# Summing the last 512 columns of the PEER value rows on TensorE

## The chip, the core and the metric

One Trainium2 chip, one of its cores. TensorE (PE) multiplies matrices into PSUM, its accumulation memory of eight banks of 512 fp32 columns; VectorE (DVE) and ScalarE (ACT) compute along the free dimension of 128 partitions; GpSimd (POOL) issues the gathers from HBM, SyncE (SP) the plain loads. All transfers share 16 DMA engines. The metric is the device time of one launch in microseconds (us), the median of three runs.

## The reference

Two layers, an S5 mixer and an RG-LRU mixer, each followed by a PEER channel mixer, over 256 prompt tokens and 32 sample tokens with 2048 channels, all in fp32. The part that matters here is the PEER mixer. Each token picks, in 8 heads, 16 of 16384 experts by product keys, and each expert is one row `u` and one row `v` of 2048:

```python
idx, g = peer_retrieve(hf, w_q, sub_keys)          # 8 heads x 16 experts, softmax weights
u = u_emb[ib]
act = jnp.einsum("nd,nhkd->nhk", xb, u)            # a dot product per expert
wgt = jax.nn.gelu(act, approximate=False) * gb
v = v_emb[ib]
out = jnp.einsum("nhk,nhkd->nd", wgt, v)           # a weighted sum of value rows
```

## The kernel before

**Tiles.** The tokens lie in three tiles: 0 and 1 are the 128-token halves of the prompt, 2 holds the 32 sample tokens, each on four partitions. A token of tiles 0 and 1 has 128 experts (PICKS) on its own partition; a sample token's 128 experts are shared out over its four copies, 32 on each, and `sample_sum` adds the copies on TensorE afterwards.

**Gathers.** POOL gathers one row of 2048 fp32 for each of the 128 partitions at a time (an indirect DMA, 1 MB) into a ring of eight slots (`ring`, in the tensor `arena`). `rounds` (L487) loops over rounds of eight gathers; slot r is filled anew when the semaphore `row_used[r]` tells that VectorE has used it. Each layer has 144 dot rows and 144 value rows in each of two halves: 288 gathers per table and layer, 1152 in all.

**Stages.** VectorE goes through the rows in one fixed order: dot rows of tiles 0 and 2, value rows of tiles 0 and 2, dot rows of tile 1, value rows of tile 1, all of layer 0; then the same for layer 1. A dot row (`u_row`, L1494) is one instruction of 2048 columns. A value row (`v_row`, L1509) multiplies the gathered row by the token's weight and adds the running sum, which lies in PSUM banks 4 to 7 (`high_banks`); each waits for the one before it, by `row_used`.

**What runs between the rows.** `Turns` counts VectorE's rows and runs other work at fixed row numbers. Two chains of work take the RG-LRU layer and the second layer's retrieval along under the rows of the PEER mixer: `first_chain` (tiles 0 and 2) under the dot rows and value rows of layer 0's tile 1, `second_chain` (tile 1) under layer 1's dot rows of tiles 0 and 2 (160 rows) and the value rows after them. The tables at the top of the file give the row numbers: NORM_ROW for the norm ahead of the queries, CHOOSE_ROW for choosing experts (`chain_choose`, three parts, two rows apart), SOFT_ROW for the softmax. Choosing takes the sixteen best of each key list and then of their sums, and turns them into expert numbers.

**TensorE.** It runs the chain's products as soon as their inputs are there (`chain`): gates and recurrence inputs, output rows (`token_rows`), then the 16 query products and four blocks of scores (`pair_scores`). The weights come as slabs of 1 MB through a ring of four slots (`W`); SP loads a slot anew when the product that read it is done. TensorE has no part in the value rows.

**Clock.** The profile's PEclk is the granted TensorE clock: 1.0 is 2.4 GHz and 0.5 is 1.2 GHz, and a stretch shows the mean.

## Time and profile before

| | us |
|---|---|
| median of 3 runs (4014.38 to 4015.89) | 4015.09 |
| the profiled execution | 4012.11 |
| its span in the profile | 4010.2 |
| VectorE busy, 84% of the span | 3371.5 |
| GpSimd busy, 39% | 1552.0 |
| TensorE busy, 30% | 1221.7 |
| ScalarE busy, 11% | 460.3 |
| bytes moved, over the whole span | 1404 MB, 350 GB/s |

The span runs from the first instruction to the last; the execution's time has 1.9 us around it. The first 690 us are the S5 layer and the first retrieval, with few transfers; from there to the end the eight slots are filled without a pause in the program. The stages in the trace, by the lines of VectorE's rows: value rows of layer 0, tiles 0 and 2, from 1121 to 1518; dot rows of tile 1 with the first chain from there to 1946; value rows of tile 1 to 2372; dot rows of layer 1 with the second chain to 2891; value rows of tiles 0 and 2 to 3374; dot rows of tile 1 to 3684; value rows of tile 1 to the end. An engine's busy share over the whole span mixes these stages, so the windows by stage are the view to read. In them the DMA column is the mean busy share of the 16 DMA engines (1.01 is full) and GB/s what they moved.

### The profile page before, as it was taken

The page shows a single profiled execution, that of the slowest core. Times are in us where ns is not written, and L with a number is a line of the kernel's source. Part 1 is how long each engine was busy: PE and PEld are TensorE (multiplying, and loading weights), DVE is VectorE, ACT ScalarE, POOL GpSimd, SP SyncE. Part 2 cuts the span into 40 slices and gives each one's busy share as a digit, 9 for nine tenths or more (in the row PEclk, how much of TensorE's full clock was granted, in tenths as well). Part 3 has the DMA queues.
Part 4 walks back from the last instruction along what each step waited for, and adds up shares of the span by engine and source line. Part 5 has one row for each costly group of instructions (what it writes and reads, how often), then busy time and mean ns, then how long its engine had stood idle before and what let it go on. Part 6 is the DMA issues. An engine that isn't in the chain of part 4 may idle for free.

```text
span 4010.2 us, 25596 instructions
## 1 busy us (share of the span) xinstructions
PE 1221.7 (30%) x7394; PEld 1015.7 (25%) x7394; DVE 3371.5 (84%) x3564; ACT 460.3 (11%) x917; POOL 1552.0 (39%) x2027
## 2 busy tenths in 40 slices
PE   4666999000000007659370026470051000000000
PEld 2333778000000006559260026460051000000000
DVE  6777026999999998896889997868979999999998
ACT  6554021000000002120000002100000000000000
POOL 5999003543433343222322342223422334434332
PEclk8878999555555558779685558785576555555555
DMA  1001335899999999999996999999997999999998
GB/s 69 13 10 51 111 126 189 334 421 399 427 427 427 427 427 407 426 426 426 419 426 237 411 423 425 427 426 426 427 427 273 374 420 417 427 427 428 427 428 367
DMA packets 197389, 1404.25 MB, mean 350 GB/s; under 512 B 21952, under 2 KB 26304, under 8 KB 26768
## 3 DMA queue, kind: packets, MB, share of 16 engines
q0 software_dynamic: 167008, 1215.18, 72.7%
q1 hardware_dynamic: 30000, 187.74, 11.6%
q8 instruction: 47, 0.77, 0.1%
q14 instruction: 46, 0.38, 0.0%
q10 hardware_dynamic: 288, 0.18, 0.0%
HBM read 1399.77 MB, written 3.24 MB: 350 GB/s over the span
## 4 chain that ended last, share of the span: by engine, by line
DVE 50%; DMA 28%; POOL 7%; PE 7%; issue 7%; ACT 1%; POOLq 0%; DVEq 0%; ACTq 0%
DVE ps L1509 30%; DMA arena<-in_u_dram,ixs 24%; DVE arena L1494 13%; DMA arena<-in_v_dram,ixs 4%; PE ps L604 3%; POOL arena L423 2%; PE ps L644 2%; POOL arena L426 1%; POOL arena L430 1%; POOL arena L431 1%; POOL arena L404 1%; DVE arena L1389 1%; DVE arena L1382 1%; POOL arena L427 1%; DVE arena L1383 1%
## 5 line engine op out<-in xcount | busy, mean ns | idle before, releaser
L1494 DVE CUSTOM_DVE_ANT_0 arena<-arena,ps 128x2048 f32<-128x2048 f32 x556 | 1254.9, 2285 | 184.8 <-DMA arena<-in_u_dram,ixs 170.3
L1509 DVE SCALAR_TENSOR_TENSOR ps<-arena,ps 128x2048 f32<-128x2048 f32 x564 | 1327.9, 2354 | 90.5 <-DMA arena<-in_v_dram,ixs 29.8
L497 POOL DMA_INDIRECT arena<-in_v_dram,ixs x576 | 566.1, 983 | 1025.7 <-DVE ps L1509 960.2
L497 POOL DMA_INDIRECT arena<-in_u_dram,ixs x560 | 545.1, 973 | 1056.4 <-DVE arena L1494 983.2
L762 PE MATMUL ps<-HT,W 128*128 128x160 f32 (+1 forms) x3072 | 407.6, 296 | 62.5 <-ACT HN L1108 28.7
L762 PEld LDWEIGHTS ps<-HT,W 128*128 128x128 f32 x3072 | 401.1, 199 | 68.6 <-issue 47.2
L741 PE MATMUL ps<-ident,HN 128*128 128x128 f32 (+1 forms) x96 | 18.8, 377 | 1304.0 <-DVE HN L1237 1304.0
L741 PEld LDWEIGHTS ps<-ident,HN 128*128 128x128 f32 (+1 forms) x96 | 15.6, 217 | 1307.8 <-DVE HN L1237 1306.2
L1331 DVE TENSOR_TENSOR_SCAN arena<-arena 128x256 f32<-128x256 f32 x128 | 84.3, 717 | 67.9 <-POOL arena L451 65.9
L710 PE MATMUL ps<-HN,arena 128*32 128x256 f32 x512 | 140.9, 443 | 0.0
L790 PE MATMUL ps<-W,arena 128*128 128x128 f32 x1024 | 125.4, 284 | 44.8 <-DVE arena L1605 20.4
L790 PEld LDWEIGHTS ps<-W,arena 128*128 128x128 f32 x1024 | 121.9, 199 | 47.2 <-DVE arena L1605 20.6
L644 PE MATMUL ps<-HT,W 128*128 128x288 f32 x512 | 126.7, 409 | 0.0
L669 PE MATMUL ps<-HN,repsum 128*128 128x512 f32 x16 | 11.8, 898 | 371.5 <-DVE HN L1509 370.1
L604 PE MATMUL ps<-arena,W 128*128 128x288 f32 x512 | 124.4, 406 | 0.8 <-ACT arena L938 0.8
L863 ACT ACTIVATE HN<-X 128x2048 f32<-128x2048 f32 x15 | 28.5, 1902 | 823.2 <-DVE X L1509 810.4
L1371 DVE TENSOR_TENSOR arena<-arena 128x288 f32 x16 | 7.3, 459 | 131.1 <-ACT arena L1007 131.1
L423 POOL TENSOR_TENSOR arena<-arena 128x32 f32<-128x32 f32 (+1 forms) x256 | 107.7, 451 | 8.9 <-POOL arena L431 8.9
L644 PEld LDWEIGHTS ps<-HT,W 128*128 128x128 f32 x512 | 97.7, 192 | 27.6 <-issue 1.0
L604 PEld LDWEIGHTS ps<-arena,W 128*128 128x128 f32 x512 | 97.2, 190 | 27.7 <-issue 1.0
L669 PEld LDWEIGHTS ps<-HN,repsum 128*128 128x128 f32 x16 | 4.2, 282 | 378.1 <-issue 373.7
L774 PE MATMUL ps<-HN,W 128*128 128x160 f32 (+1 forms) x256 | 53.6, 379 | 101.1 <-ACT HN L1120 99.3
(245 smaller groups left out, 2171.2 us busy)
## 6 DMA issues: line engine op xcount, KB each, us to landing
W<-in_slabs_dram SPq DMA_DIRECT2D x168, 1024.0 KB, 10.8
arena<-in_u_dram,ixs POOLq DMA_INDIRECT x576, 16.5
arena<-in_v_dram,ixs POOLq DMA_INDIRECT x576, 14.3
GB<-in_norms_dram POOLq DMA_DIRECT2D x4, 1024.0 KB, 6.0
arena<-in_s_bc_dram SPq DMA_DIRECT2D x32, 128.0 KB, 2.1
X<-in_x_dram SPq DMA_DIRECT2D x3, 1024.0 KB, 10.8
out_y_dram<-HN SPq DMA_DIRECT2D x2, 1024.0 KB, 6.6
arena<-in_keys_dram POOLq DMA_DIRECT2D x1, 1024.0 KB, 5.2
```

What stands on the lines that cost most here:

```text
L404: ins = nc.gpsimd.tensor_tensor(t[n], b[c], f[e], ALU.mult)
L423: ins = nc.gpsimd.tensor_tensor(t[n], a[c], s[e], ALU.mult)
L497: pool.indirect_dma_start(ring[:, r, :], None, table, bass.IndirectOffsetOnAxis(ap=ixs[:, side, r:r + 1], axis=0)).then_inc(row_in[r], 16)
L604: mm = nc.tensor.matmul(ps[:, r % 2, 0:NT], W[:, slot, P * k:P * (k + 1)], rhs[:, k, :], start=(k == 0), stop=(k == KT - 1))
L644: mm = nc.tensor.matmul(ps[:, r % 2, 0:NT], W[:, slot, P * k:P * (k + 1)], HT[:, k, :], start=(k == 0), stop=(k == KT - 1))
L710: nc.tensor.matmul(ps[rows, 5, 0:SEQ], c, PR[n][:, q, :], start=False, stop=(n == 3), skip_group_check=True)
L762: mm = nc.tensor.matmul(ps[:, bank, 0:CHAIN_COLS[c]], W[:, slot, P * k:P * (k + 1)], HT1[c][:, k, :], start=(k == 0), stop=(k == KT - 1))
L774: mm = nc.tensor.matmul(ps[:, bank, 0:CHAIN_COLS[c]], W[:, slot, at:at + P], XC[c][g % 2][:, 2 * (b // 4) + e, :], start=(e == 0), stop=(e ...
L790: mm = nc.tensor.matmul(ps[:, bank, out], Y[:, k, :], W[:, slot, P * k:P * (k + 1)], start=(k == 0), stop=(k == KT - 1))
L1331: ins = V.tensor_tensor_scan(dst[:, q, :], dec[:, bass.ds(k * QK + q, 1)].to_broadcast([P, SEQ]), src[:, q, :], 0.0, ALU.mult, ALU.add)
L1494: V.tensor_tensor_reduce(ring[:, r, :], ring[:, r, :], token, 1.0, 0.0, ALU.mult, ALU.add, AV[:, COL_AT[t] + n:COL_AT[t] + n + 1]).then_in ...
L1509: V.scalar_tensor_tensor(to, ring[:, r, :], weight, total, ALU.mult, ALU.add).then_inc(row_used[r], 1)
```

## The change

VectorE's value row is cut to the first 1536 columns (OWN). For the other 512, VectorE writes the token's weight on the diagonal of a 128 x 128 matrix (DG, three buffers, from `ident`), and TensorE multiplies that matrix with the row's last 512 columns and accumulates in PSUM bank 7 over all rows of a tile (`value_rows`). At a tile's end VectorE adds the bank to X or copies it to ACC (`last_columns`), and `v_done` takes the place of the last `row_used` for those who wait for the sum.

A slot may now be filled only when both engines have read it, so POOL waits for `row_used[r]` and `row_pe[r]` in value rounds (`value_rounds`). Ahead of the dot rounds that follow value rows it waits once for all eight `row_pe` (`values_read`), at three places.

On TensorE the value rows stand in one instruction order with the chain: the query products of a chain, with their transposes and scores, are taken out of `chain` and placed between value rows by a `Turns` of TensorE's own (TURN_ROW). CHOOSE_ROW and SOFT_ROW move to later rows and further apart.

```diff
+OWN = D - BANK
+DIAGS = 3
+PHASES = [(0, 0), (0, 2), (0, 1), (1, 0), (1, 2), (1, 1)]
-NORM_ROW = [132, 172]
-CHOOSE_ROW = [[150, 158, 166, 174, 180], [190, 198, 206, 214]]
-SOFT_ROW = [192, 224]
+NORM_ROW = [132, 168]
+TURN_ROW = [6, 10]
+CHOOSE_ROW = [[158, 170, 182, 194, 202], [196, 208, 220, 232]]
+SOFT_ROW = [212, 244]
...
+def values_before(layer, t):
+    return sum(PICKS_OF[u] for _, u in PHASES[:PHASES.index((layer, t))])
...
+            def value_rounds(layer, t):
+                start, at = ROUNDS * layer + V_AT[t], ROUNDS * layer + V_AT[t] - COL_AT[t] // RING
+                before = values_before(layer, t) // RING
+                with pool.Fori(start // 2, start // 2 + PICKS_OF[t] // RING // 2) as i:
+                    for side in range(2):
+                        indices(at, i, side)
...
+                        for r in range(RING):
+                            pool.wait_ge(row_used[r], i * 2 + side)
+                            pool.sem_inc(gather_go, 1)
+                            pool.wait_ge(row_pe[r], i * 2 + (side + before + 1 - start))
+                            pool.sem_inc(gather_go, 1)
+                            issue(experts_v[layer], i, side, r)
+
+            def values_read(rounds):
+                for r in range(RING):
+                    pool.wait_ge(row_pe[r], rounds + 1)
...
+            value_rounds(0, 0)
+            value_rounds(0, 2)
+            values_read(values_before(0, 1) // RING)
+            dot_rounds(experts_u[0], U_AT[1] - PITCH // RING, U_AT[1], V_AT[1])
+            value_rounds(0, 1)
...
+            def chain_queries(c):
+                yield TURN_ROW[c]
                 if c == 0:
                     turned(8, 0)
+                    yield TURN_ROW[c] + 2
                     turned(9, 2)
...
                 for p in range(4):
                     for i in range(4):
+                        yield TURN_ROW[c] + 6 + 3 * (4 * p + i)
                         chain_product(c, LOAD_Q + 4 * p + i, MM_Q + 4 * p + i)
                         if i == 0 and p > 0:
                             pair_scores(c, p - 1)
+                yield TURN_ROW[c] + 6 + 3 * 16
                 pair_scores(c, 3)
...
+            def value_rows(layer, t, turns):
+                first = values_before(layer, t)
+                if first > 0:
+                    pe.wait_ge(v_done, PHASES.index((layer, t)))
+                for n in range(PICKS_OF[t]):
+                    R, r = ROUNDS * layer + V_AT[t] + n // RING, n % RING
+                    pe.wait_ge(diag_set, first + n + 1)
+                    pe.wait_ge(row_in[r], 16 * (R + 1))
+                    nc.tensor.matmul(ps[:, 7, :], DG[(first + n) % DIAGS], ring[:, r, OWN:D], start=(n == 0),
+                                     stop=(n == PICKS_OF[t] - 1)).then_inc(row_pe[r], 1)
+                    turns.row()
...
             chain(0)
+            turns = Turns(chain_queries(0))
+            value_rows(0, 1, turns)
+            turns.finish()
...
             def v_row(layer, t, n):
...
+                v = values_before(layer, t) + n
+                if v >= DIAGS:
+                    dve.wait_ge(row_pe[(v - DIAGS) % RING], (v - DIAGS) // RING + 2)
+                V.tensor_scalar(DG[v % DIAGS], ident[:], weight, None, ALU.mult).then_inc(diag_set, 1)
                 dve.wait_ge(row_in[r], 16 * (R + 1))
...
+                row = ring[:, r, 0:OWN]
...
-                V.scalar_tensor_tensor(to, ring[:, r, :], weight, total, ALU.mult, ALU.add).then_inc(row_used[r], 1)
+                V.scalar_tensor_tensor(to, row, weight, total, ALU.mult, ALU.add).then_inc(row_used[r], 1)
+
+            def last_columns(layer, t):
+                dve.wait_ge(row_pe[RING - 1], (values_before(layer, t) + PICKS_OF[t]) // RING + 1)
+                if t == 2:
+                    V.tensor_copy(ACC[:, OWN:D], ps[:, 7, :]).then_inc(v_done, 1)
+                else:
+                    V.tensor_tensor(X[:, t, OWN:D], ps[:, 7, :], X[:, t, OWN:D], ALU.add).then_inc(v_done, 1)
```

Three places in the order of instructions show what moves. The first is TensorE at the end of the first chain (HT and W are the chain's tokens and the weight slabs, `arena` with 128x512 a ring slot's last columns). Before, after the transposes:

```order
L741 MATMUL ps<-ident,HN 128x128 x16
L741 MATMUL ps<-ident,HN 128x32 x16
L762 MATMUL ps<-HT,W 128x160 x80
L806 MATMUL ps<-HT,arena 128x128
L808 MATMUL ps<-HT,arena 32x128
```

And now:

```order
L905 MATMUL ps<-arena 128x512 x6
L783 MATMUL ps<-ident,HN 128x128 x16
L905 MATMUL ps<-arena 128x512 x2
L783 MATMUL ps<-ident,HN 128x32 x16
L905 MATMUL ps<-arena 128x512 x4
L804 MATMUL ps<-HT,W 128x160 x16
L905 MATMUL ps<-arena 128x512 x3
L804 MATMUL ps<-HT,W 128x160 x16
L905 MATMUL ps<-arena 128x512 x3
```

Five query products stood in one run of 80 matmuls; now one of 16 comes after every three value rows.

The second place is VectorE at the start of a tile's value rows, with the waits of each instruction (`arena` is the slot, X the first running sum, `ident` the source of the diagonal). Before:

```order
L1509 SCALAR_TENSOR_TENSOR ps<-arena,X 128x2048 [waits row_in0,vstep]
L1509 SCALAR_TENSOR_TENSOR ps<-arena,ps 128x2048 [waits row_used0,row_in1]
L1509 SCALAR_TENSOR_TENSOR ps<-arena,ps 128x2048 [waits row_used1,row_in2]
L1509 SCALAR_TENSOR_TENSOR ps<-arena,ps 128x2048 [waits row_used2,row_in3]
L1509 SCALAR_TENSOR_TENSOR ps<-arena,ps 128x2048 [waits row_used3,row_in4]
```

And now, in layer 0's tile 1:

```order
L1587 TENSOR_SCALAR arena<-ident,arena 128x128 [waits row_pe5,vstep]
L1597 SCALAR_TENSOR_TENSOR ps<-arena,X 128x1536 [waits row_in0]
L1587 TENSOR_SCALAR arena<-ident,arena 128x128 [waits row_pe6]
L1597 SCALAR_TENSOR_TENSOR ps<-arena,ps 128x1536 [waits row_used0,row_in1]
L1587 TENSOR_SCALAR arena<-ident,arena 128x128 [waits row_pe7]
L1597 SCALAR_TENSOR_TENSOR ps<-arena,ps 128x1536 [waits row_used1,row_in2]
```

Ahead of each sum stands a diagonal, which waits for TensorE's product of three rows earlier and not for its own row.

The third place is POOL between the last value rows and the next dot rows, here at the end of layer 1's tile 2. Before:

```order
L497 DMA arena<-in_v_dram,ixs 128x2048 [waits row_used7]
L489 REGISTER_ALU
L489 COMPARE_AND_BRANCH
L489 UNCONDITIONAL_BRANCH [waits chain_picks]
L489 ISA
L484 COPY ixs<-arena 128x8
L492 ISA
L497 DMA arena<-in_u_dram,ixs 128x2048 [waits index_set,row_used0]
L497 DMA arena<-in_u_dram,ixs 128x2048 [waits row_used1]
```

And now:

```order
L502 DMA arena<-in_v_dram,ixs 128x2048 [waits row_used7,row_pe7]
L521 REGISTER_ALU
L521 COMPARE_AND_BRANCH
L507 UNCONDITIONAL_BRANCH [waits row_pe4,row_pe3,row_pe5,row_pe2,row_pe6,row_pe1,row_pe7,row_pe0,chain_picks]
L507 ISA
L497 COPY ixs<-arena 128x8
L510 ISA
L502 DMA arena<-in_u_dram,ixs 128x2048 [waits index_set,row_used0]
L502 DMA arena<-in_u_dram,ixs 128x2048 [waits row_used1]
```

The first dot gather, which waited for its own slot alone, now stands behind TensorE's reads of all eight.

## Rows read from the trace of the kernel before

**Rows 1.** The page's chain of waits, part 4: shares of the span by engine.

```profile
DVE 50%; DMA 28%; POOL 7%; PE 7%; issue 7%; ACT 1%; POOLq 0%; DVEq 0%; ACTq 0%
```

**Rows 2.** Windows by stage: busy us per engine, PEclk, DMA share, GB/s.

```profile
1121.00:1518.00 397.00, 3.64 (x16) 3.00 (x16) 379.80 (x169) 5.94 (x9) 155.79 (x179) 0.50 1.01 427
1526.00:1946.00 420.00, 294.35 (x2192) 289.79 (x2192) 349.89 (x464) 64.58 (x181) 119.36 (x134) 0.84 1.01 421
1946.00:2372.00 426.00, 96.21 (x608) 87.19 (x608) 392.97 (x448) 15.69 (x34) 140.29 (x151) 0.60 0.92 377
2372.00:2891.00 519.00, 215.61 (x1680) 208.65 (x1680) 417.66 (x444) 65.43 (x148) 165.11 (x180) 0.72 1.01 426
2891.00:3374.00 483.00, 71.37 (x561) 69.29 (x562) 439.44 (x408) 16.03 (x33) 163.91 (x180) 0.57 0.93 382
...
3684.00:3994.00 310.00, 0.00 (x0) 0.00 (x0) 295.91 (x127) 0.05 (x1) 119.15 (x136) 0.50 1.01 426
```

**Rows 3.** Instruction groups: busy us, mean ns of one; idle before, releasers.

```profile
L1509 DVE SCALAR_TENSOR_TENSOR ps<-arena,ps 128x2048 f32<-128x2048 f32 x564 | 1327.9, 2354 | 90.5 <-DMA arena<-in_v_dram,ixs 29.8 <-DVE arena L1389 5.1 <-DVE ps L1509 2.8
L1494 DVE CUSTOM_DVE_ANT_0 arena<-arena,ps 128x2048 f32<-128x2048 f32 x556 | 1254.9, 2285 | 184.8 <-DMA arena<-in_u_dram,ixs 170.3 <-DVE arena L1429 0.2
...
L1338 DVE SCALAR_TENSOR_TENSOR HN<-arena 128x1024 f32<-128x1024 f32 x16 | 20.4, 1278 | 0.0
```

**Rows 4.** VectorE's timeline, a choice of experts: start us, us, line, operation.

```profile
2067.98 0.89 DVE L1379 MAX8 arena<-ps 128x8 f32<-128x128 f32 x4
...
2073.86 4.82 DVE L1509 SCALAR_TENSOR_TENSOR ps<-arena,ps 128x2048 f32<-128x2048 f32 x2 [0.31 <-DVE arena L1389]
2078.59 0.19 DVE L1413 CAST arena<-arena 128x64 f32<-128x64 uint32 x1
...
2084.25 4.82 DVE L1509 SCALAR_TENSOR_TENSOR ps<-arena,ps 128x2048 f32<-128x2048 f32 x2 [0.22 <-DVE arena L1389]
2088.98 0.17 DVE L1420 TENSOR_SCALAR arena<-arena 128x32 uint32<-128x32 uint32 x1
...
2093.55 9.72 DVE L1509 SCALAR_TENSOR_TENSOR ps<-arena,ps 128x2048 f32<-128x2048 f32 x4
```

**Rows 5.** Line L1557 (ns min/median/max), then the timeline of all engines there.

```profile
L1557 DVE TENSOR_SCALAR HN<-HN,CH x32: 333/343/499, 1564.1 to 2564.0; 128x128 f32<-128x128 f32 x32
...
1564.13 0.34 DVE L1557 TENSOR_SCALAR HN<-HN,CH 128x128 f32<-128x128 f32 x1
1564.39 0.30 DVE L1561 TENSOR_SCALAR HN<-HN,CH 128x32 f32<-128x32 f32 x1
...
1565.02 0.95 POOL L497 DMA_INDIRECT arena<-in_u_dram,ixs  x1 [3.97 <-DVE arena L1494]
```

**Rows 6.** TensorE's timeline (PE, PEld): sums of the samples, then query products.

```profile
3373.69 3.52 PE L669 MATMUL ps<-HN,repsum 128*128 128x512 f32 x4 [307.49 <-DVE HN L1509]
3378.63 1.98 PE L669 MATMUL ps<-HN,repsum 128*128 128x512 f32 x4 [1.41 <-DVE X L1540]
...
3373.66 0.50 PEld L669 LDWEIGHTS ps<-HN,repsum 128*128 128x128 f32 x2 [307.76 <-issue]
...
2038.72 17.65 PE L762 MATMUL ps<-HT,W 128*128 128x160 f32 x128
...
2930.40 18.13 PE L762 MATMUL ps<-HT,W 128*128 128x128 f32 x160 [0.69 <-ACT HT L1086]
```

**Rows 7.** A refill by POOL (timeline), landing times of gathers, windows after value stages.

```profile
1520.93 0.19 POOL L484 COPY ixs<-arena 128x8 int32 x1
...
1522.04 0.97 POOL L497 DMA_INDIRECT arena<-in_u_dram,ixs  x1 [0.91 <-POOL ixs L484]
...
DMA to landing us min/median/max: 5.4/16.0/36.3
...
1530.00:1550.00 20.00, 15.31 (x100) 15.10 (x101) 19.96 (x19) 2.44 (x14) 9.73 (x10) 0.74 0.90 333
3390.00:3410.00 20.00, 0.00 (x0) 0.00 (x0) 19.96 (x19) 0.00 (x0) 9.30 (x9) 0.50 0.97 386
```

More of the change, by code:

```diff
@@ L232, in hybrid_step @@
         cube = [P, PAIR, TOPK, TOPK]
+        OH1 = view(RING * D + 10 * PITCH + 40 + 256, 2 * PAIR * CANDS)
+        DG = [view(at - 512 + P * n, P) for n in range(DIAGS)]
         LIN = view(at, 512)
@@ L293, in hybrid_step @@
         row_used = [sem(f"row_used{r}") for r in range(RING)]
+        row_pe = [sem(f"row_pe{r}") for r in range(RING)]
+        diag_set, v_done = sem("diag_set"), sem("v_done")
         hn_set, index_set, gather_go = sem("hn_set"), sem("index_set"), sem("gather_go")
@@ L485, in indices, with issue, dot_rounds @@
                                       ).then_inc(index_set, 1)
-            def rounds(table, at, start, end):
+            def issue(table, i, side, r):
+                pool.indirect_dma_start(ring[:, r, :], None, table,
+                                        bass.IndirectOffsetOnAxis(ap=ixs[:, side, r:r + 1], axis=0)).then_inc(row_in[r], 16)
+            def dot_rounds(table, at, start, end):
                 with pool.Fori(start // 2, end // 2) as i:
@@ L496, in rounds @@
                             pool.sem_inc(gather_go, 1)
[L497 to L499 removed]
+                            issue(table, i, side, r)
+            def value_rounds(layer, t):
[4 more added lines that the diff above has]
+                        indices(at, i, side)
+                        pool.wait_ge(index_set, i * 2 + (side + 1))
+                        pool.sem_inc(gather_go, 1)
[3 more added lines that the diff above has]
+                            pool.wait_ge(row_pe[r], i * 2 + (side + before + 1 - start))
+                            pool.sem_inc(gather_go, 1)
+                            issue(experts_v[layer], i, side, r)
+            def values_read(rounds):
+                for r in range(RING):
+                    pool.wait_ge(row_pe[r], rounds + 1)
             def one_head(h, par):
@@ L839, in chain, with sample_turn @@
                             pair_scores(c, p - 1)
+                yield TURN_ROW[c] + 6 + 3 * 16
                 pair_scores(c, 3)
-            turned(6, 0)
+            def sample_turn():
+                yield 8
+                turned(6, 0)
+            def value_rows(layer, t, turns):
[9 more added lines that the diff above has]
+                    turns.row()
+            value_rows(0, 0, Turns(()))
+            turns = Turns(sample_turn())
+            value_rows(0, 2, turns)
+            turns.finish()
             pe.wait_ge(norm_ht, 28)
@@ L846, in _ @@
             chain(0)
+            turns = Turns(chain_queries(0))
+            value_rows(0, 1, turns)
+            turns.finish()
             turned(10, 1)
             chain(1)
+            turns = Turns(chain_queries(1))
+            value_rows(1, 0, turns)
+            turns.finish()
+            value_rows(1, 2, Turns(()))
             pe.wait_ge(key_used, 2 + HEADS + 8)
             sample_sum(1)
+            value_rows(1, 1, Turns(()))
         @block.scalar
@@ L1181, in _ @@
             chain_queries(0)
-            token_bank(0, ROUNDS, 9)
+            act.wait_ge(v_done, 3)
+            token_bank(0, 9)
             square(10, 1)
@@ L1210, in _ @@
             st = Steps()
+            for r in range(RING):
+                dve.sem_inc(row_pe[r], 1)
             dve.sem_inc(key_used, 2)
@@ L1503, in v_row @@
                     dve.wait_ge(row_used[(n - 1) % RING], ROUNDS * layer + V_AT[t] + (n - 1) // RING + 1)
+                row = ring[:, r, 0:OWN]
                 if n == 0 and t == 2:
-                    V.tensor_scalar(high_banks, ring[:, r, :], weight, None, ALU.mult).then_inc(row_used[r], 1)
+                    V.tensor_scalar(high_banks[:, 0:OWN], row, weight, None, ALU.mult).then_inc(row_used[r], 1)
                     return
-                total = X[:, t, :] if n == 0 else high_banks
-                to = high_banks if n < PICKS_OF[t] - 1 else ACC if t == 2 else X[:, t, :]
-                V.scalar_tensor_tensor(to, ring[:, r, :], weight, total, ALU.mult, ALU.add).then_inc(row_used[r], 1)
+                total = X[:, t, 0:OWN] if n == 0 else high_banks[:, 0:OWN]
+                to = high_banks[:, 0:OWN] if n < PICKS_OF[t] - 1 else ACC[:, 0:OWN] if t == 2 else X[:, t, 0:OWN]
+                V.scalar_tensor_tensor(to, row, weight, total, ALU.mult, ALU.add).then_inc(row_used[r], 1)
[5 more added lines that the diff above has]
+                    V.tensor_tensor(X[:, t, OWN:D], ps[:, 7, :], X[:, t, OWN:D], ALU.add).then_inc(v_done, 1)
             def u_rows(layer, t, turns, hn_count):
```

64 lines of the change are left out of this document (32 added, 32 removed).

## The prediction, made before the changed kernel was run

> **What bounds the kernel now.** I read the chain of waits first, then the busy times stage by stage, and only then single instructions. The chain gives half of the span to VectorE and 28% to transfers, and its largest piece is the value row on L1509 [rows 1]. Taken alone that promises much for a shorter value row. The stages say otherwise [rows 2]. One gathered row is 128 x 2048 x 4 bytes = 1.0486 MB; at 427 GB/s it takes 2.456 us. In the first value stage (1121 to 1518) the transfer engines are busy throughout at 427 GB/s, in the last one (3684 to 3994) at 426, and in the stages of dot rows and recurrence (1526 to 1946, 2372 to 2891) at 421 and 426. There a faster VectorE can only wait longer for rows.
>
> Two stages are different: 1946 to 2372 moved 377 GB/s and 2891 to 3374 moved 382. In bytes not moved that is (1 - 377/427) x 426 = 49.9 us and (1 - 382/427) x 483 = 50.9 us, **100.8 us** together. In them VectorE chooses experts between value rows. One choice has three parts; their starts and the starts of the next value rows give 5.88 + 5.66 + 4.57 = 16.1 us [rows 4]. The value row itself has no slack to pay for that: it lasts 2.354 us [rows 3], and four in a row take 9.72, a pitch of (9.72 - 2.35)/3 = 2.456 us [rows 4], exactly a row's transfer. So five choices (80.5 us) and four choices (64.4 us) come out as lost transfer, less what lies ready in the ring of eight: 80.5 - 49.9 = 30.6 and 64.4 - 50.9 = 13.5 us. The first also contains the last weight slabs, which moved while VectorE was late; the second holds few of them. I take the ring alone as 11 us (8 to 17; eight rows less the one in use are 17).
>
> **The change, part by part.** *Shorter value row.* From 1024 columns (1.278 us) to 2048 (2.354 us) an element costs 1.051 ns [rows 3]; 1536 columns give 1.278 + 512 x 1.051 = 1.816 us. The added diagonal is a TENSOR_SCALAR of 128 x 128 with a weight per partition. Its nearest rows are the 32 on L1557: median 343 ns, and the next instruction starts 0.26 us after one starts [rows 5]. The old pitch contains 0.10 us in which a row waits for its predecessor's result; the diagonal now stands in that gap. Without such a wait the next instruction started 4.73 us after the first of two value rows, so 4.73 - 2.456 = 2.27, or 0.08 before the row's end [rows 4]. New pitch: 1.816 - 0.08 + 0.26 = **2.00 us**. Lower bound: the old gap, with the diagonal wholly inside, 1.92. Upper bound: nothing overlaps, 1.816 + 0.343 + 0.10 = 2.26. I take 2.00, because both instructions on L1557's stretch overlap in that way.
>
> That leaves 2.456 - 2.00 = 0.456 us a row for choosing. *Choices spread out.* In the first chain they start at value row 30 and the softmax is at 84 (turn rows 158 and 212, less the 128 dot rows); the query products on TensorE stand at value rows 12, 15, ..., 57, and each frees a slot for one slab. Ten slabs are moved from row 30 on, 24.6 us of transfer during which VectorE may lag. Loss: 80.5 - 54 x 0.456 - 24.6 - 11 = 20.3 us. In the second chain (160 dot rows ahead) it is rows 36 to 84 and five slabs: 64.4 - 48 x 0.456 - 12.3 - 11 = 19.2 us. Together 39.5, plus 6 for TensorE's share of the pace (below): 46 instead of 100.8, a gain of **55 us**. With 1.92 and a cushion of 17 the two losses fall to 10 and 9 (a gain of 81); with 2.26 they are 34 and 32 (a gain of some 29 after TensorE's 6).
>
> *A barrier for the gathers.* Before, a slot's first dot row was issued as soon as that slot's value row was used. Now POOL waits, at three places, until TensorE has read the last value row, and all eight gathers of the next stage stand behind that wait; the dot rows on VectorE wait for them. When the last value row has landed nothing is in flight. TensorE's product of 512 columns takes 1.76 us at the slower level (3.52 for two) and 0.99 at the faster, with weights ahead of it (two loads in 0.50) [rows 6]: about 2.0. Then come POOL's index copy and its wait, 1.1 us, and the issue, 0.97 [rows 7]. The shortest landing was 5.4 us from issue; less 0.97 for issuing and 2.456 for moving, 2.0 us pass before data flows [rows 7]. Idle transfer: 2.0 + 1.1 + 1.0 + 2.0 = 6.1 us, three times, 18. Two of these places already lose (1 - 333/427) x 20 = 4.4 and (1 - 386/427) x 20 = 1.9 us, since VectorE stalls there on sums of the samples [rows 7]; that stall now lies beside the refill. Net cost 12 us (8 to 18).
>
> *TensorE's rows.* 576 products of at most 1.76 us plus weights lie inside a row's 2.456 us and beside VectorE's 1.82. The diagonal is built before the row lands, so both engines start at landing, and the slot comes free no later than before (2.35). Nothing for this, except where query products stand between. VectorE may build three diagonals ahead; if TensorE falls further behind, the fourth waits, and behind it on VectorE the sum and any choice, for which POOL waits in turn.
>
> *Query products in line.* A product of the first chain takes 17.65/4 = 4.41 us at the faster level, of the second 18.13/5 = 3.63 [rows 6]. Twelve value rows and four products make 12 x 1.27 + 17.6 = 32.9 us of TensorE in the first chain, against 16 transfers x 2.456 = 39.3: it fits, with the score products narrowly (hence the 6 us). *Ends of stages.* The last 512 columns are added by one 0.69 us instruction; it is exposed only at the very end, some 1 us.
>
> *A rule against the change.* L1557's instructions ran while POOL issued a gather (0.95 us from 1565.02); the longest of the 32 took 499 ns, and POOL's issue stayed at its usual length [rows 5]. The Trainium skill, "SBUF — State Buffer", section "Who interferes with whom", says that a tensor_scalar can take a two-port mode on ports shared with GpSimd, and that whichever issues first blocks the other fully. By the rows an encounter costs up to 0.16 us; by the rule it could cost the whole issue, and the sum would be rival 3's.
>
> **Sum.** Profiled execution: 4012.1 us (span 4010.2). 4012.1 - 55 + 12 + 1 = 3970; the median of the three runs is 3.0 above the profiled one, so **3973 us**, 1.0% faster. What a measurement can tell from no change is 0.2%, 8 us.
>
> **Rivals.**
> 1. *The spreading hides nearly all choices.* With pitch 1.92 and the full ring the gain is 81, the barriers cost 8: 4015 - 81 + 8 + 1 = 3943. For it: VectorE's idle time before rows is small, so whatever is saved is used. Against it: from row 60 on no slabs come, and two choices plus softmax stand in 24 rows, with 11 us of slack.
> 2. *TensorE becomes the bound, slower than before.* Its queue is in order: a value row stands behind each query product. At the slower level twelve rows and four products take 12 x 2.0 + 35.3 = 59.3 us in the first chain and 24 + 29.0 = 53 in the second, against 39.3. Over 48 rows each that loses 80 and 55 us, less two cushions, and the choices after row 60 still cost about 30: 143 in place of 100.8. With the barriers 4015 + 42 + 12 = 4069. In time at the slower level s, the first chain is late from (39.3 - 32.9)/26.4 = a quarter; the run turns slower than before at about six tenths. For it: in the two stages the granted clock was 0.60 and 0.57. Against it: there TensorE was busy 96 of 426 us; in 1526 to 1946 it was busy 294 of 420 and got 0.84 [rows 2], and value rows make this stretch denser still, the more so the slower it runs.
> 3. *POOL's issue holds up every diagonal.* If each waited 0.95 us, the pitch would be 2.95, above the transfer, in all 576 rows: 576 x 0.49 = 282 us and about 4300. The 499 ns above speak against it; a smaller dose (pitch 2.26) ends near 4015 - 29 + 12 + 1 = 3999.
> 4. *All 576 rows pay.* 576 x 0.456 = 263 us would give 3752. The 427 GB/s of the pure value stages exclude it, as bytes are unchanged.
>
> **How the numbers follow.** Forecast (3955 to 3990) 0.60; rival 1 0.12; pitch near 2.26, 3990 to 4010, 0.10, nearly all of it faster; gain eaten up by barriers and TensorE together, within 8 us of 4015, 0.05; rival 2 0.11; rival 3 in full 0.02. Faster 0.80, same 0.06, slower 0.14. The range runs from rival 1 to the dear diagonal, 3937 to 4012; outside lie rivals 2 and 3, most of the no-change case and a tail below, 0.2 in all.
>
> **What the profile after would show.** Value rows of 1.82 us and diagonals of about 0.34; a pitch near 2.0 where choices stand, still 2.456 in the first and last value stages; 405 GB/s or more in the two stages of choices; three gaps of about 6 us in the gathers ahead of dot rows, with POOL waiting for TensorE; TensorE at the faster level between value rows 12 and 60. The forecast is wrong if VectorE waits there for TensorE's products (rival 2), if diagonals take 0.5 us or more (rival 3), or if the gaps last beyond 10 us.

## The result, and the profile after

The changed kernel takes 3975.24 us (median of four runs, 3974.68 to 3975.65), against 4014.74 for the kernel before beside it: a ratio of 0.9903 (0.9886 to 0.992), 1.0% faster. The profiled execution's span fell from 4010.2 to 3973.2 us. The forecast was 3973.

The chain of waits has turned round. Where VectorE held 50% and transfers 28% [rows 1], the page after shows this (part 4, then part 5's group of the new value row: busy us, mean ns of one, idle before and its releaser):

```profile
DMA 50%; DVE 24%; PE 11%; POOL 7%; issue 7%; ACT 1%; POOLq 0%; DVEq 0%; ACTq 0%
...
L1597 DVE SCALAR_TENSOR_TENSOR ps<-arena,ps 128x1536 f32<-128x1536 f32 x564 | 1027.9, 1823 | 207.3 <-DMA arena<-in_v_dram,ixs 206.9
```

The value row lasts 1.823 us where it was 2.354 [rows 3], and of its 207.3 us of idle time 206.9 are waits for a row. Two value rows and the diagonal between them on VectorE's timeline, ahead of the third part of a choice:

```profile
2072.46 1.81 DVE L1597 SCALAR_TENSOR_TENSOR ps<-arena,ps 128x1536 f32<-128x1536 f32 x1
2074.19 0.28 DVE L1587 TENSOR_SCALAR arena<-ident,arena 128x128 f32<-128x128 f32 x1
2074.39 1.82 DVE L1597 SCALAR_TENSOR_TENSOR ps<-arena,ps 128x1536 f32<-128x1536 f32 x1
```

The second sum starts 1.93 us after the first (2.456 before [rows 4]): the diagonal starts 0.09 before the sum ends and the next sum 0.20 after the diagonal.

The stages, in windows as in [rows 2] (us; busy us of PE, PEld, DVE, ACT, POOL; PEclk, DMA share, GB/s): a stage of value rows alone, then the two stages with choices, and between them a piece of the first:

```profile
1122.00:1505.00 383.00, 278.65 (x328) 69.73 (x328) 316.16 (x321) 5.66 (x8) 148.66 (x171) 0.64 1.01 427
1965.00:2337.00 372.00, 266.10 (x856) 139.17 (x856) 324.49 (x558) 15.65 (x34) 124.19 (x138) 0.76 0.97 397
2190.00:2250.00 60.00, 30.61 (x36) 8.20 (x36) 57.54 (x122) 0.34 (x1) 17.95 (x20) 0.64 0.76 283
2880.00:3313.00 433.00, 301.90 (x872) 135.90 (x872) 372.45 (x560) 15.50 (x32) 155.24 (x172) 0.77 0.98 409
```

Value rows alone run at 427 GB/s as before. The stages with choices went from 377 and 382 to 397 and 409. In transfer not done that is (1 - 397/427) x 372 = 26.1 and (1 - 409/427) x 433 = 18.3 us, 44.4 in place of 100.8: a gain of 56.4. What is left lies close together: 2190 to 2250 lost (1 - 283/427) x 60 = 20.2 us, the first chain's last two choices and its softmax.

The three joints between value rows and dot rows, and the end (same columns), of after and then of before:

```profile
1505.00:1560.00 55.00, 34.99 (x152) 23.93 (x151) 43.96 (x44) 7.04 (x22) 23.98 (x24) 0.72 0.83 346
2337.00:2390.00 53.00, 30.46 (x174) 23.43 (x173) 40.32 (x38) 9.25 (x19) 25.99 (x23) 0.67 0.89 369
3313.00:3370.00 57.00, 15.37 (x16) 4.14 (x16) 44.52 (x44) 5.37 (x5) 24.57 (x24) 0.54 0.88 364
3940.00:3973.20 33.20, 16.15 (x19) 3.89 (x18) 21.17 (x21) 3.49 (x4) 1.89 (x2) 0.60 0.59 249
```

```profile
1510.00:1560.00 50.00, 31.64 (x182) 27.44 (x183) 46.06 (x41) 7.84 (x28) 21.57 (x20) 0.73 0.96 388
2365.00:2390.00 25.00, 5.47 (x33) 4.87 (x34) 24.65 (x20) 7.78 (x10) 14.31 (x11) 0.56 1.00 409
3370.00:3410.00 40.00, 5.51 (x8) 1.85 (x8) 39.07 (x36) 5.37 (x5) 19.03 (x18) 0.59 0.99 406
3977.00:4010.20 33.20, 0.00 (x0) 0.00 (x0) 24.49 (x13) 3.49 (x4) 1.89 (x2) 0.50 0.58 244
```

They lose 10.4, 7.2 and 8.4 us, 26.0 together, where the kernel before lost 4.6, 1.1 and 2.0: 18.4 us more. The end loses 13.8 instead of 14.2. Sum: 4010.2 - 56.4 + 18.4 - 0.4 = 3971.8, and the span is 3973.2. The 1.4 us left fit a later start: the first dot row begins at 696.75 where it began at 694.68.

Inside the second joint (all engines; the last value row, its product, POOL's index copy and first gather; then windows of 1 us):

```profile
2345.53 1.81 DVE L1597 SCALAR_TENSOR_TENSOR X<-arena,ps 128x1536 f32<-128x1536 f32 x1 [0.43 <-DMA arena<-in_v_dram,ixs]
...
2345.64 1.10 PE L905 MATMUL ps<-arena 128*128 128x512 f32 x2 [0.46 <-DMA arena<-in_v_dram,ixs]
2347.09 0.19 POOL L497 COPY ixs<-arena 128x8 int32 x1 [17.23 <-PE ps L905]
...
2348.18 0.96 POOL L502 DMA_INDIRECT arena<-in_u_dram,ixs  x1 [0.90 <-POOL ixs L497]
```

```profile
2343.00:2344.00 1.00, 0.80 (x1) 0.50 (x2) 0.91 (x1) 0.00 (x0) 0.00 (x0) 0.50 0.47 197
2344.00:2345.00 1.00, 1.00 (x2) 0.00 (x0) 1.00 (x2) 0.00 (x0) 0.00 (x0) 0.51 0.06 25
...
2349.00:2350.00 1.00, 0.00 (x0) 0.00 (x0) 0.00 (x0) 1.00 (x2) 0.70 (x2) 0.50 0.25 49
2350.00:2351.00 1.00, 0.00 (x0) 0.00 (x0) 0.00 (x0) 1.00 (x1) 0.69 (x2) 0.50 0.93 188
```

The transfers fall off at 2343.5, two microseconds before the last value row can start at 2345.53. The 25 GB/s after that are a sixteenth of 427: in the trace's packet records one of the 16 engines runs on after the others, with one packet of 8 KB every 0.31 us until 2345.18, and the last value row starts 0.35 us later. The first packets of the dot rows begin at 2349.85, 1.67 us after the issue at 2348.18, and between 2350 and 2351 the transfers still run at 188 GB/s.

### The profile page after: what moved, and what is told of

It reads as the page before. It is cut to its first block, busy times and chain, and to the rows that moved or that the text cites. A ratio compares the mean times of both kernels' runs of the same rounds, so it can differ in the third digit from the quotient of the medians.

```text
span 3973.2 us, 29731 instructions
## 1 busy us (share of the span) xinstructions
PE 2155.2 (54%) x8546; PEld 1261.4 (32%) x8546; DVE 3169.4 (80%) x4146; ACT 459.7 (12%) x917; POOL 1547.0 (39%) x2027
## 3 DMA queue, kind: packets, MB, share of 16 engines
q1 hardware_dynamic: 30000, 187.74, 11.7%
## 4 chain that ended last, share of the span: by engine, by line
DMA 50%; DVE 24%; PE 11%; POOL 7%; issue 7%; ACT 1%; POOLq 0%; DVEq 0%; ACTq 0%
DMA arena<-in_u_dram,ixs 26%; DMA arena<-in_v_dram,ixs 23%; DVE arena L1577 12%; DVE ps L1597 6%; PE ps L646 3%; PE ps L905 3%; POOL arena L436 3%; PE ps L686 2%; POOL arena L439 1%; POOL arena L444 1%; PE ps L804 1%; POOL arena L443 1%; DVE arena L1472 1%; DVE arena L1465 1%; DVE arena L1466 1%
## 5 line engine op out<-in xcount | busy, mean ns | idle before, releaser
L905 PE MATMUL ps<-arena 128*128 128x512 f32 x1152 | 943.6, 923 | 1367.2 <-DVE arena L1587 1096.1
L1597 DVE SCALAR_TENSOR_TENSOR ps<-arena,ps 128x1536 f32<-128x1536 f32 x564 | 1027.9, 1823 | 207.3 <-DMA arena<-in_v_dram,ixs 206.9
L502 POOL DMA_INDIRECT arena<-in_v_dram,ixs x576 | 557.9, 969 | 959.6 <-PE ps L905 656.7
L905 PEld LDWEIGHTS ps<-arena 128*128 128x128 f32 x1152 | 241.3, 258 | 2030.0 <-DVE arena L1587 1417.9
L804 PE MATMUL ps<-HT,W 128*128 128x160 f32 (+1 forms) x3072 | 420.0, 300 | 74.8 <-ACT arena L1187 32.0
L804 PEld LDWEIGHTS ps<-HT,W 128*128 128x128 f32 x3072 | 415.8, 203 | 101.1 <-issue 85.2
L1587 DVE TENSOR_SCALAR arena<-ident,arena 128x128 f32<-128x128 f32 x576 | 164.5, 286 | 9.7 <-PE ps L905 5.8
L436 POOL TENSOR_TENSOR arena<-arena 128x32 f32<-128x32 f32 (+1 forms) x256 | 116.6, 485 | 8.9 <-POOL arena L444 8.9
L686 PEld LDWEIGHTS ps<-HT,W 128*128 128x128 f32 x512 | 97.9, 192 | 27.6 <-issue 1.0
L744 PE MATMUL ps<-HT,arena 128*128 (+1 forms) x32 | 19.4, 710 | 129.1 <-POOL arena L444 129.1
```

Of the source, the lines that this page charges most:

```text
L436: ins = nc.gpsimd.tensor_tensor(t[n], a[c], s[e], ALU.mult)
L502: pool.indirect_dma_start(ring[:, r, :], None, table, bass.IndirectOffsetOnAxis(ap=ixs[:, side, r:r + 1], axis=0)).then_inc(row_in[r], 16)
L686: mm = nc.tensor.matmul(ps[:, r % 2, 0:NT], W[:, slot, P * k:P * (k + 1)], HT[:, k, :], start=(k == 0), stop=(k == KT - 1))
L804: mm = nc.tensor.matmul(ps[:, bank, 0:CHAIN_COLS[c]], W[:, slot, P * k:P * (k + 1)], HT1[c][:, k, :], start=(k == 0), stop=(k == KT - 1))
L905: nc.tensor.matmul(ps[:, 7, :], DG[(first + n) % DIAGS], ring[:, r, OWN:D], start=(n == 0), stop=(n == PICKS_OF[t] - 1)).then_inc(row_pe[r ...
L1587: V.tensor_scalar(DG[v % DIAGS], ident[:], weight, None, ALU.mult).then_inc(diag_set, 1)
```

## The experiments

Each was run beside the kernel before; ratios are to it, with their 95% interval, and differences are taken from medians.

### The new row numbers alone

```diff
 (kernel before)
-NORM_ROW = [132, 172]
-CHOOSE_ROW = [[150, 158, 166, 174, 180], [190, 198, 206, 214]]
-SOFT_ROW = [192, 224]
+NORM_ROW = [132, 168]
+CHOOSE_ROW = [[158, 170, 182, 194, 202], [196, 208, 220, 232]]
+SOFT_ROW = [212, 244]
```

> The kernel before with nothing but the new row numbers of NORM_ROW, CHOOSE_ROW and SOFT_ROW; VectorE keeps all 2048 columns. My theory: a value row of 2.456 us pitch leaves nothing over for choices, wherever they stand, and only the ring and the slabs hide some of them. The two stages lose about 101 us of transfer as before: 4015 us (4007 to 4023). Rival, the spreading is what gained the 56 us and TensorE's columns are a bystander: the losses fall to some 45 us and the time to about 3959.

Measured: 4020.65 us, ratio 1.0017 (1.0008 to 1.0027). The windows of its two stages, in the profiled execution (4013.71 us, the fastest of ten):

```profile
1962.00:2373.00 411.00, 99.56 (x608) 89.30 (x608) 372.56 (x432) 13.19 (x31) 130.50 (x143) 0.60 0.91 368
2895.00:3373.00 478.00, 70.03 (x560) 68.07 (x560) 436.28 (x405) 15.03 (x30) 163.54 (x179) 0.57 0.93 383
```

They lose 56.8 + 49.3 = 106 us, no less than before, and the median is 7 us longer. Spreading without a shorter value row gains nothing.

### The widest table alone

```diff
 (kernel before)
+NORM_ROW = [132, 168]
+CHOOSE_ROW = [[154, 166, 182, 204, 226], [190, 204, 222, 256]]
+PART_ROWS = [[4, 5, 7, 7, 8], [4, 5, 8, 8]]
+SOFT_ROW = [248, 284]
...
-                yield row + 2
+                yield row + PART_ROWS[c][step]
...
-                yield row + 4
+                yield row + 2 * PART_ROWS[c][step]
```

> The kernel before with the widest table of all: choices at 26, 38, 54, 76, 98 and 30, 44, 62, 96, their parts 4 to 8 rows apart; VectorE keeps all 2048 columns, and the slotwise refill is what that kernel has anyway. With 1536 columns on VectorE the same table ran in 3925 us. My theory: at a pitch of 2.456 us, equal to the transfer, the ring is empty after the first choice and nothing fills it again but the slabs, so the distance between choices is worth nothing: 4015 us (4007 to 4024), some 100 us lost in the two stages. Rival, a full ring ahead of each part hides it and the table alone gives most of the gain: 3960 or less.

Measured: 4020.97 us, ratio 1.0019 (1.001 to 1.0029). This is the table with which the fastest kernel below runs.

```profile
1962.00:2373.00 411.00, 100.60 (x608) 90.34 (x608) 372.99 (x434) 15.68 (x34) 130.96 (x143) 0.60 0.92 371
2895.00:3373.00 478.00, 72.62 (x560) 70.50 (x560) 435.03 (x408) 15.72 (x32) 162.75 (x179) 0.57 0.94 383
```

53.9 + 49.3 = 103 us lost: the two wider tables gain no more than the old one. A pitch equal to the transfer leaves nothing with which to fill the ring again.

### TensorE's columns with the choices close together

```diff
 (changed kernel)
-NORM_ROW = [132, 168]
-CHOOSE_ROW = [[158, 170, 182, 194, 202], [196, 208, 220, 232]]
-SOFT_ROW = [212, 244]
+NORM_ROW = [132, 172]
+CHOOSE_ROW = [[150, 158, 166, 174, 180], [190, 198, 206, 214]]
+SOFT_ROW = [192, 224]
...
-                        yield TURN_ROW[c] + 6 + 3 * (4 * p + i)
+                        yield TURN_ROW[c] + 6 + 2 * (4 * p + i)
...
-                yield TURN_ROW[c] + 6 + 3 * 16
+                yield TURN_ROW[c] + 6 + 2 * 16
```

> The changed kernel with its choices as close as they stood before: the old NORM_ROW, CHOOSE_ROW and SOFT_ROW, and the query products two value rows apart where they were three, so that the scores are there in time. My theory: TensorE's columns give the slack of 0.536 us a row, the rows between the first choice and the softmax say how much of it is used; 12 and 14 rows fewer cost 0.536 x 26 = 14 us, less what slabs that come closer together hide: 3986 us (3978 to 3996). Rival, the spreading carries most of the gain, slack or not: the losses go back to about 100 us and the time to 4015 or more, since the barriers stay. A second rival, TensorE's queue with denser query products becomes the bound: VectorE waits for products, 4000 or more, with the waits for TensorE named in the trace.

Measured: 3991.33 us, ratio 0.9945 (0.9928 to 0.9961).

```profile
1970.00:2350.00 380.00, 280.84 (x857) 136.05 (x858) 323.31 (x558) 15.66 (x34) 125.02 (x136) 0.76 0.95 386
2892.00:3330.00 438.00, 311.08 (x870) 131.63 (x870) 371.97 (x561) 15.71 (x32) 154.33 (x172) 0.74 0.97 403
```

The stages lose 36.5 + 24.6 = 61.1 us, 16.7 more than in the changed kernel, and the time is 16.1 longer. So of the gain of 56.4 us about 40 come with the choices as close as before, and 17 with the new distances of choices and query products, those only on top of the shorter row.

Not all of the 17 is shown to be distance between choices. The product of three rows earlier held up four diagonals for 7.1 us in all, against 5.8 in the changed kernel. But VectorE also waited for scores (us in total, times, longest):

```profile
DVE arena L1462 <- PE ps L850: 11.9, 3, 6.1
```

Three choices of the first chain were held up until TensorE had finished their scores, at 2040, 2074 and 2109; in the changed kernel none was. That stage loses 10.4 us more than in the changed kernel, and how much of this the late scores cost stays open: here the second rival is partly at work. The second stage has no such wait and loses 6.3 us more.

### A dearer diagonal

```diff
 (changed kernel)
+                if v >= 1:
+                    dve.wait_ge(extra_set, v)
+                V.tensor_scalar(zeros[:], zeros[:], weight, None, ALU.mult).then_inc(extra_set, 1)
                 V.tensor_scalar(DG[v % DIAGS], ident[:], weight, None, ALU.mult).then_inc(diag_set, 1)
```

> The changed kernel with a second TENSOR_SCALAR of 128 x 128 ahead of every diagonal (zeros times the weight, written back to zeros; nothing reads a result of it), so that VectorE's pitch rises by some 0.2 us to 2.12 in all 576 value rows. My theory: a row's cost on VectorE counts only where choices stand, because elsewhere the row's transfer of 2.456 us sets the pace; the two losses of 26 and 19 us grow by 18 together: 3993 us (3985 to 4002). Rival, every value row pays: 576 x 0.2 = 115 us, about 4090.

Measured: 4000.16 us, ratio 0.9966 (0.9955 to 0.9978), 24.9 us more than the changed kernel.

```profile
1125.00:1505.00 380.00, 274.87 (x325) 68.12 (x325) 342.06 (x468) 5.66 (x8) 149.35 (x170) 0.64 1.01 427
1970.00:2350.00 380.00, 264.83 (x858) 135.88 (x858) 345.47 (x680) 15.13 (x33) 122.99 (x136) 0.78 0.95 388
2893.00:3335.00 442.00, 297.38 (x872) 135.02 (x872) 400.30 (x715) 14.27 (x30) 155.16 (x172) 0.78 0.97 400
```

In the stage of value rows alone VectorE is busy 342 of 380 us instead of 316 of 383, and the transfers stay at 427 GB/s: the extra 0.2 us a row costs nothing there. The stages with choices lose 34.7 + 27.9 = 62.6 us, 18.2 more, the 18 that were expected. Of the other 7 us, the three joints take 2.7 and the end 2.2 (28.8 and 16.0 us lost instead of 26.0 and 13.8); the rest I did not pursue.

### A refill slot by slot

```diff
 (changed kernel, dot_rounds)
                             pool.wait_ge(row_used[r], i * 2 + side)
                             pool.sem_inc(gather_go, 1)
+                            if read is not None:
+                                pool.wait_ge(row_pe[r], read + 1)
+                                pool.sem_inc(gather_go, 1)
                             issue(table, i, side, r)
...
-            values_read(values_before(0, 1) // RING)
-            dot_rounds(experts_u[0], U_AT[1] - PITCH // RING, U_AT[1], V_AT[1])
+            dot_rounds(experts_u[0], U_AT[1] - PITCH // RING, U_AT[1], V_AT[1], values_before(0, 1) // RING)
```

(and in the same way at the other two places)

> The changed kernel, but POOL waits ahead of each dot gather for TensorE's read of that slot alone, no longer for all eight at once. My theory: the three pauses in the transfers between value rows and dot rows, 24.2 us together, shrink to the 5.2 us they were before: 3956 us (3951 to 3962), and the choices lose 45 us as they do now. Rival, VectorE's stall on the sums of the samples takes the place of the barrier at two of the three places: only the third pause goes, about 3968.

Measured: 3954.23 us, ratio 0.9853 (0.9836 to 0.9869), 21.0 us less than the changed kernel. The three joints:

```profile
1505.00:1560.00 55.00, 41.70 (x219) 32.49 (x219) 47.03 (x46) 8.36 (x32) 23.35 (x22) 0.81 1.01 423
2327.00:2380.00 53.00, 36.04 (x220) 27.20 (x221) 43.40 (x40) 9.93 (x23) 24.32 (x21) 0.76 1.01 426
3298.00:3355.00 57.00, 12.57 (x17) 3.65 (x16) 51.76 (x52) 5.37 (x5) 24.99 (x24) 0.62 1.01 427
```

They lose 0.5 + 0.1 + 0 us: the pauses are gone, and VectorE's stall on the sums of the samples no longer stops the transfers, so the rival falls. Of the 25.4 us saved, 21 reach the end; the stages with choices lose 45.8 us here instead of 44.4, and the end 16.4 instead of 13.8.

### Choices farther apart

```diff
 (changed kernel)
-CHOOSE_ROW = [[158, 170, 182, 194, 202], [196, 208, 220, 232]]
-SOFT_ROW = [212, 244]
+CHOOSE_ROW = [[154, 166, 182, 208, 234], [190, 204, 222, 260]]
+SOFT_ROW = [246, 280]
```

> The changed kernel with the choices at other rows: 26, 38, 54, 80, 106 of the 128 value rows in the first chain (softmax 118) and 30, 44, 62, 100 of 160 in the second (120); the query products and the barrier stay. My theory: the 45 us still lost come from choices standing closer than 0.536 us a row of slack plus the slabs can pay, most of them behind the last slab; farther apart they lose 6 to 14 us together: 3939 us (3932 to 3950). Rival, the loss comes from TensorE's queue (query products ahead of value rows) or from interference of POOL with the diagonals: moving the choices gains under 10 us, 3965 to 3975.

Measured: 3956.65 us, ratio 0.9857 (0.984 to 0.9873): 18.6 us less than the changed kernel, half of what I expected, and above the range. Its two stages, and in each a window around one choice that stands alone:

```profile
1969.00:2325.00 356.00, 255.79 (x855) 135.68 (x855) 317.33 (x552) 14.56 (x33) 123.47 (x136) 0.81 0.99 411
2290.00:2310.00 20.00, 12.45 (x16) 3.21 (x16) 19.72 (x25) 0.34 (x1) 7.31 (x8) 0.68 0.90 346
2870.00:3295.00 425.00, 296.88 (x872) 134.72 (x871) 370.67 (x560) 13.09 (x28) 153.07 (x171) 0.77 0.99 415
3065.00:3095.00 30.00, 17.27 (x24) 4.58 (x24) 29.39 (x42) 0.00 (x0) 10.69 (x12) 0.77 0.87 345
```

The stages lose 13.3 + 11.9 = 25.2 us, of which 3.8 and 5.8 lie around these two choices. A choice that stands alone still overruns the ring: 16.1 us, less 4 x 0.536 that the rows between its parts give back, less the 4 to 6 lost, leaves 8 to 10 us that eight slots hide. The prediction's 11 us for the ring would have given 3 us a choice; my 6 to 14 for all nine had let the slack of later rows count for it.

### Both together

> The slotwise wait and the wider choices together. My theory: the two losses lie in different stretches of the program, so the gains add: 3920 us (3912 to 3930). Rival, a full ring at the end of one stage only moves the wait to the next: less than two thirds of the sum, 3935 or more.

Measured: 3938.33 us, ratio 0.9811 (0.9794 to 0.9827). 21.0 + 18.6 = 39.6 us were to be had by the two runs before this, and 36.9 came: the gains add. The expected 3920 was missed by what the wide table alone had missed; the time lies in the rival's range, but its condition, less than two thirds of the sum, is not met.

### The parts of a choice apart

The slotwise refill, and the table and PART_ROWS of the run of the widest table:

> The slotwise wait and wider choices (26, 38, 54, 76, 98 and 30, 44, 62, 96), and the three parts of a choice 4 to 8 rows apart where they were 2. My theory: of the 25 us that the wider choices still lose, nearly all is lost within single choices, since 16.1 us less 4 x 0.536 is more than the 10 us that eight slots hold; parts 7 or 8 rows apart stay within the ring: 3918 us (3910 to 3927). Rival, what is left comes from the query products in TensorE's queue or from VectorE's lag behind TensorE: no less than with the parts two rows apart, 3935 to 3940.

Measured: 3924.90 us, ratio 0.9779 (0.9763 to 0.9795). The two stages:

```profile
1961.00:2325.00 364.00, 255.24 (x864) 133.73 (x864) 327.19 (x564) 15.66 (x34) 130.44 (x144) 0.84 1.00 415
1985.00:2125.00 140.00, 118.99 (x584) 85.80 (x583) 120.21 (x211) 5.05 (x17) 45.37 (x51) 0.91 0.99 411
2849.00:3278.00 429.00, 300.94 (x880) 136.08 (x880) 378.65 (x568) 15.16 (x30) 162.19 (x180) 0.77 1.01 425
```

They lose 10.2 + 2.0 = 12.2 us. With four to eight rows between its parts a choice hardly overruns the ring, so the reading of the run with the wider table holds; the last choices also stand up to four rows closer than there, which if anything cost time. Half of the 10.2 us, (1 - 411/427) x 140 = 5.2, lies over the query products, where one choice waits 4.2 us for its scores. This is the fastest version: 2.2% below the kernel before and 1.3% below the change.

### 1024 columns on TensorE

```diff
 (changed kernel)
-OWN = D - BANK
+OWN = D - 2 * BANK
...
-                    nc.tensor.matmul(ps[:, 7, :], DG[(first + n) % DIAGS], ring[:, r, OWN:D], start=(n == 0),
-                                     stop=(n == PICKS_OF[t] - 1)).then_inc(row_pe[r], 1)
+                    for b in range(2):
+                        mm = nc.tensor.matmul(ps[:, 6 + b, :], DG[(first + n) % DIAGS],
+                                              ring[:, r, OWN + BANK * b:OWN + BANK * (b + 1)], start=(n == 0),
+                                              stop=(n == PICKS_OF[t] - 1))
+                    mm.then_inc(row_pe[r], 1)
```

> The changed kernel with 1024 columns on TensorE and 1024 on VectorE (OWN smaller by 512; two products a row with the same diagonal, in banks 6 and 7). VectorE's pitch falls to about 1.4 us, TensorE's work for a row doubles: 4.1 us at the slower level, 2.1 at the faster, against 2.456 of transfer. My theory: TensorE without pauses is granted the faster level most of the time, as in the stretch 1526 to 1946 of the kernel before (0.84), so the stages of value rows alone stay at about the transfer's pace; the stretches with query products are bound by TensorE (three rows and a product 10.8 us against 9.8) and lose 15 to 30 us there, the choices lose 10 instead of 45: 3965 us (3945 to 4010). Rival, the granted clock stays where it is in those stages (0.63): a row takes 3.3 us there, 432 x 0.8 = 350 us more, about 4300.

Measured: 3959.79 us, ratio 0.9866 (0.9849 to 0.9882), 15.4 us less than the change. TensorE's timeline in a stage of value rows, first of the changed kernel and then of this one, then windows of that stage and of the two stages with choices:

```profile
1305.93 2.05 PE L905 MATMUL ps<-arena 128*128 128x512 f32 x2 [0.84 <-DMA arena<-in_v_dram,ixs]
```

```profile
1306.10 1.96 PE L906 MATMUL ps<-arena 128*128 128x512 f32 x4 [0.49 <-DMA arena<-in_v_dram,ixs]
```

```profile
1125.00:1500.00 375.00, 300.28 (x629) 106.88 (x628) 228.86 (x310) 5.66 (x8) 148.18 (x170) 0.99 1.01 427
1969.00:2325.00 356.00, 317.88 (x1097) 173.74 (x1098) 255.55 (x554) 15.39 (x34) 120.49 (x136) 0.96 0.99 406
2874.00:3292.00 418.00, 359.46 (x1176) 178.49 (x1176) 290.77 (x556) 14.54 (x30) 151.95 (x172) 0.96 1.00 419
```

The rival with a slow clock falls: the granted clock rose from 0.64 to 0.99, and a row's two products take 1.96 us, where the one product of the changed kernel took 2.05 near 1306 (at a granted clock of 0.50 from 1305 to 1317.5). Over the whole stage TensorE is busy 300 of 375 us instead of 279 of 383, a tenth more of the time for twice the work. The choices lose 17.5 + 7.8 = 25.3 us, 19 less than in the change.

### 1024 columns and the parts apart

> The slotwise wait, the wider choices with their parts 4 to 8 rows apart, and 1024 columns on TensorE. My theory: with parts apart the choices lose only 12 us, most of it at the start of the first chain and not for want of slack on VectorE; a cheaper value row has little left to gain, and TensorE without a pause beside the query products takes some back: 3921 us (3912 to 3932). Rival, VectorE's value row is still what limits: 3912 or less.

Measured: 3936.61 us, ratio 0.9808 (0.9791 to 0.9824): 11.7 us slower than with 512 columns, and above the range. The stretch of the query products, and VectorE's waits (us in total, times, longest):

```profile
1985.00:2125.00 140.00, 132.10 (x586) 88.47 (x585) 88.31 (x199) 4.44 (x15) 39.87 (x44) 0.95 0.94 374
```

```profile
DVE arena L1591 <- PE ps L907: 70.1, 54, 7.6
```

From 1985 to 2125 TensorE is busy 132 of 140 us and the transfers run at 374 GB/s, where they ran at 411 with 512 columns: 17.4 us lost instead of 5.2. VectorE waits 33.3 us for products in this stretch, and 70.1 in the whole execution. Here, with twice the work, my second rival's mechanism is at work, at the faster level of the clock.

## Why the prediction was right

**Where the time lies: right.** The prediction put all of the gain into the two stages with choices and none into the others. The dearer diagonal shows it: 0.2 us more in every row moved nothing in the stage of value rows alone.

**The pitch: 1.92 instead of 2.00, the lower bound.** The diagonal takes 280 ns in the median where 343 was the nearest row [rows 5], and the next instruction starts 0.20 after it.

**The choices: 55 forecast, 56.4 measured, by two errors that cancel.** With the pitch of 1.92 the prediction's own sum leaves 80.5 - 54 x 0.536 - 24.6 - 11 = 16.0 and 64.4 - 48 x 0.536 - 12.3 - 11 = 15.4 us, with TensorE's 6 together 37; 44.4 are lost. The step that failed is the slack counted over a whole stretch against the sum of its choices. Slack that comes after the ring is full is lost, and a choice longer than the ring loses at once. The first chain's last two choices stand 8 rows apart, and 8 x 0.536 = 4.3 us do not pay for 16.1. The prediction's sign of 405 GB/s or more is missed in this stage, at 397, and met in the other, at 409. Runs with the choices closer (late scores included), wider, and with their parts apart left 61.1, 25.2 and 12.2 us.

**The barriers: 12 forecast, 18.4 measured, just past the upper bound of 18.** The step that failed is the count of 6.1 us from "when the last value row has landed nothing is in flight": idle transfer was counted from that landing on, but the engines run dry before it. At this place they fall off 2 us ahead, as one engine runs on alone, and the first gather fills them slowly. From the landing on, the pause is shorter than forecast, 4.3 us from 2345.53 to the first packet (5.3 at the other two places): the product took 1.10 us, at a granted clock of 1.00, where about 2.0 were forecast (2.04 at the other two places); copy with its wait (1.09) was as forecast; and from the start of the issue to the first packet 1.67 us passed where 0.97 + 2.0 were forecast. The Trainium skill, "DMA: Bandwidth & Descriptors", section "Anatomy of one DMA — SWDGE (gpsimd) path", says that of a fixed cost of about 2.0 us most is the wait until the last byte is confirmed. The 2 us ahead of 2345.53 are not such a wait: the last packet ends 0.35 us before the row starts. At the first place, too, a single engine runs on, until 1513.18, 2.4 us longer than the others, and the row starts 0.33 us after it; 10.4 us are lost there, just past the 10 that the prediction named as its sign of being wrong. Why one engine falls behind stays open.

**TensorE: right, with room.** The queue cost little, as this line of VectorE's waits of the changed kernel shows:

```profile
DVE arena L1587 <- PE ps L905: 5.8, 4, 1.9
```

The granted clock over the query products, which decided rival 2, was high. The window over them in the first chain:

```profile
2000.00:2160.00 160.00, 133.81 (x638) 98.77 (x639) 135.25 (x270) 4.55 (x15) 47.88 (x55) 0.86 1.00 415
```

At 0.86 the stretch loses (1 - 415/427) x 160 = 4.5 us; 6 were forecast for both chains. 0.86 is (1 - 0.86)/0.5 = 0.28 of the time at the slower level, just past the quarter from which the prediction had the chain late, and far from the six tenths that the rival needed.

**POOL and the diagonals: right, at the lower bound.** The line of the diagonal (ns min/median/max), one of the few long diagonals with POOL's issue across it, then one of the usual length, early in an issue:

```profile
L1587 DVE TENSOR_SCALAR arena<-ident,arena x576: 266/280/482, 1122.6 to 3959.3; 128x128 f32<-128x128 f32 x192
```

```profile
2084.01 0.94 POOL L502 DMA_INDIRECT arena<-in_v_dram,ixs  x1 [0.30 <-issue]
2084.53 0.47 DVE L1587 TENSOR_SCALAR arena<-ident,arena 128x128 f32<-128x128 f32 x1
2084.73 1.93 DVE L1597 SCALAR_TENSOR_TENSOR ps<-arena,ps 128x1536 f32<-128x1536 f32 x1
```

```profile
2002.80 0.97 POOL L502 DMA_INDIRECT arena<-in_v_dram,ixs  x1 [3.28 <-PE ps L905]
2002.85 0.28 DVE L1587 TENSOR_SCALAR arena<-ident,arena 128x128 f32<-128x128 f32 x1
```

The longest of 576 diagonals took 482 ns, and the median issue of a gather is 944 ns in both kernels. An encounter lengthens the diagonal by up to 0.2 us and the sum behind it by up to 0.12, and the pitch stays below the transfer. What the diagonal waits for is the end of the issue: all 28 that took more than 330 ns start 0.51 to 0.67 us into one and end 37 to 50 ns after it, while the 18 that start within its first 0.48 us took 278 to 286. The four longest on L1557 before [rows 5] end 47 or 48 ns after an issue in the same way. The Trainium skill, "SBUF — State Buffer", section "Who interferes with whom", would have one of the two blocked for the other's whole instruction. By this trace there is a block, but a short one: only diagonals that would still run in the last part of the issue wait, and none waits out the 0.94 us.

**The end: +1 forecast, -0.4 measured.** The forecast of 3970 for the profiled execution is a span of 3968.2; it was 3973.2. The terms missed by +6.4 at the barriers and -1.4 each at choices and end, and 1.4 ahead of the value rows were not forecast: 5.0 us together. The choices' term is right only because pitch and use of the slack offset each other: that the forecast came within 3 us is luck, that it named the two stages is not.

## What to carry to other kernels

Read transfer rates by stage before pricing a shorter instruction: it pays only where the transfers pause, and there by the slack it opens, not by its own saving. Slack is worth what the buffer can hold: a block of work longer than the ring loses at once, and cutting it into parts (three here) brought 13 us more where moving it had brought 19. When a second engine comes to read a ring, let each slot be refilled as soon as its own readers are done; waiting for all eight at a stage's end cost 21 us at three places here.
